# The memory's keys and values, made in an opening stage and reloaded for attention

## The reference

```python
def memory_kv(mem, g_mem, w_mkv):
    mk, mv = split_cols(rmsnorm(mem, g_mem) @ w_mkv, (D_MODEL, D_MODEL))   # 256 x 1024 each
x = x + concat([o_dn, o_ssm]) @ w_out                  # gated delta net | Mamba2, both from rmsnorm(x, g_mix) @ w_in
x = x + memory_cross_attention(rmsnorm(x, g_xattn), mem_k, mem_v, w_xq, w_xo)   # q = c @ w_xq; softmax(q k^T / 16) v; @ w_xo
x = x + peer_ffn(rmsnorm(x, g_ffn), ...)               # 128^2 experts, top 16 of 8 heads
y = rmsnorm(x, g_final)
```

## Time and profile before

| | us |
|---|---|
| median of three runs | 5662.15 |
| profiled execution | 5645.43 |
| its span, from the first to the last instruction | 5643.6 |
| loads before the norm of x | 0 to 18.9 |
| norm of x and gates, until the delta net's first load | 18.9 to 91.5 |
| memory's keys and values | 2151.8 to 2252.8 |

### The profile page before, as it was taken

How to read it: one execution, slowest core, us unless ns; L and a number is a source line. 1 busy time by engine, 2 the same in 40 slices (tenths; PEclk the granted TensorE clock), 3 DMA queues, 4 the chain that set the end, 5 groups by cost and what they waited for, 6 DMA issues and landing times. The chain is left out here.

```text
span 5643.6 us, 75351 instructions
## 1 busy us (share of the span) xinstructions
PE 4734.4 (84%) x28237; PEld 4252.3 (75%) x28237; DVE 3211.3 (57%) x6524; ACT 1561.6 (28%) x2965; POOL 1733.4 (31%) x999
## 2 busy tenths in 40 slices
PE   5999999997878586777683666799999999999996
PEld 3777777775656485757683556799999999999996
DVE  2344444442555311221219999577778877777787
ACT  1233222222232211111200444233333333333332
POOL 0111111110111221202210434455555555555552
PEclk8999999997989798898886888899999999999998
DMA  1000000000111302141220244888888888888885
GB/s 66 24 27 27 24 23 27 27 13 35 47 39 39 141 34 82 58 148 37 94 79 25 75 134 119 283 287 291 284 290 295 289 287 289 299 287 281 289 297 194
DMA packets 299961, 802.45 MB, mean 142 GB/s; under 512 B 43584, under 2 KB 188992, under 8 KB 245696
## 3 DMA queue, kind: packets, MB, share of 16 engines
q0 software_dynamic: 55296, 402.68, 20.2%
q1 hardware_dynamic: 207552, 350.36, 18.0%
q10 hardware_dynamic: 36864, 46.15, 2.5%
HBM read 709.22 MB, written 89.89 MB: 142 GB/s over the span
## 5 line engine op out<-in xcount | busy, mean ns | idle before, releaser
L126 PE MATMUL psum_banks<-f_dense_hi,exp_u_hi 128*128 128x352 f32 x2048 | 665.7, 325 | 77.0 <-POOL exp_u_lo L2212 59.6
L2221 POOL DMA_INDIRECT residual<-in_peer_rows,pick_index x384 | 515.6, 1343 | 574.4 <-DVE psum_banks L2430 508.5
L2418 DVE CUSTOM_DVE_ANT_0 residual<-residual,f_rows 128x1024 f32<-128x1024 f32 x384 | 659.8, 1718 | 45.1 <-DMA residual<-in_peer_rows,pick_index 44.4
L126 PE MATMUL psum_banks<-exp_hidden_hi,exp_v_hi 128*128 128x352 f32 x2048 | 661.7, 323 | 7.8 <-issue 7.1
L127 PE MATMUL psum_banks<-f_dense_lo,exp_u_hi 128*128 128x352 f32 x2048 | 661.9, 323 | 0.0
L128 PE MATMUL psum_banks<-f_dense_hi,exp_u_lo 128*128 128x352 f32 x2048 | 661.7, 323 | 0.0
L127 PE MATMUL psum_banks<-exp_hidden_lo,exp_v_hi 128*128 128x352 f32 x2048 | 659.9, 322 | 0.0
L128 PE MATMUL psum_banks<-exp_hidden_hi,exp_v_lo 128*128 128x352 f32 x2048 | 659.7, 322 | 0.0
L476 PE MATMUL psum_banks<-x_normed,dn_weights 128*128 128x384 f32 (+1 forms) x1536 | 528.6, 487 | 13.1 <-DMA dn_conv_w<-in_dn_conv_w 13.1
L2430 DVE SCALAR_TENSOR_TENSOR psum_banks<-residual,exp_coefs,psum_banks 128x1024 f32<-128x1024 f32 x381 | 487.3, 1279 | 0.0
L784 POOL TENSOR_TENSOR dn_block<-dn_lower,dn_level_masks 128x1152 f32<-128x1152 f32 x56 | 146.8, 2628 | 1005.2 <-DVE dn_lower L862 892.8
(11 more groups left out here) (480 smaller groups left out, 9348.0 us busy)
## 6 DMA issues: line engine op xcount, KB each, us to landing
exp_stage<-in_peer_u SPq DMA_DIRECT2D x128, 512.0 KB, 4.8
exp_stage<-in_peer_v SPq DMA_DIRECT2D x128, 512.0 KB, 3.8
exp_gates<-expert_gates ACTq DMA_DIRECT2D x256, 176.0 KB, 4.5
expert_gates<-route_gates SPq DMA_DIRECT2D x5, 8192.0 KB, 31.2
dn_weights<-in_w_dn SPq DMA_DIRECT2D x8, 2048.0 KB, 7.3
retrieval_q<-w_pq_stage SPq DMA_DIRECT2D x16, 576.0 KB, 2.8
residual<-retrieval_q SPq DMA_DIRECT2D x9, 1024.0 KB, 5.9
heads<-mixed_heads SPq DMA_DIRECT2D x16, 544.0 KB, 8.8
```

Source lines behind the costliest of these rows:

```text
L126: nc.tensor.matmul(out, w[0], x[0], start=start, stop=False)
L2221: nc.gpsimd.indirect_dma_start(slot[:, n % SLOTS, :, :].rearrange("p x n -> p (x n)"), None, d["peer_rows"], bass.IndirectOffsetOnAxis(ap= ...
L2418: nc.vector.tensor_tensor_reduce(u, u, xg[:, g, :], 1.0, 0.0, ALU.mult, ALU.add, dots[:, r:r + 1]).then_inc(dotted.sem, 1)
```

## The change

`opening` takes the place of the first loads, the norm of x, `gates` and `memory_kv`, in one phase with one block. SyncE issues three constants, x tile by tile (a semaphore each), memory, the other constants, four pieces (512 KB each) of the keys' weight and four of the values', and then one more piece whenever TensorE has used one. The keys' products are plain float32. The values' matmuls run piece by piece of the weight, into four banks at once. Keys and values go to the outputs and once more to DRAM (`kept_k`, `kept_v`), and the phase waits for all four stores. The query projection takes the two reloads as `prefetch`, and the prompt's attention waits for them before its first scores. The norms and the gates' arithmetic are as before.

```diff
+def opening(nc, bank, xn, const, names, d, kept, tab):
+    STREAM = 4
...
+            def _(sp_):
+                for n in early:                      # ident, ones, gains
...
+                for k in range(KT):
+                    sp_.dma_start(x[:, k, :], d["xT"][k]).then_inc(x_loaded[k].sem, 16)
+                sp_.dma_start(mn[:, :, :], d["memT"]).then_inc(mem_loaded.sem, 16)
...
+                for j in range(KT):
+                    if j >= STREAM:
+                        sp_.wait_ge(k_product.sem, k_product.at(j - STREAM + 1))
+                    sp_.dma_start(wk[:, j % STREAM, :, :], d["w_mk"][j]).then_inc(wk_loaded[j % STREAM].sem, 16)
+                    if j == STREAM - 1:
+                        for k in range(STREAM):
+                            sp_.dma_start(wv[:, k, :], d["w_mv"][:, k, :]).then_inc(wv_loaded[k].sem, 16)
+                for k in range(STREAM, KT):
+                    sp_.wait_ge(v_step.sem, v_step.at(k - STREAM + 1))
+                    sp_.dma_start(wv[:, k % STREAM, :], d["w_mv"][:, k, :]).then_inc(wv_loaded[k % STREAM].sem, 16)
+                sp_.wait_ge(k_taken.sem, k_taken.at(KT))
+                for to in kept[0]:
+                    sp_.dma_start(to, kT[:, :, :]).then_inc(mem_stored.sem, 16)
+                sp_.wait_ge(v_taken.sem, v_taken.at(2 * MT))
+                for to in kept[1]:
+                    sp_.dma_start(to, v_out[:, :, :]).then_inc(mem_stored.sem, 16)
+                sp_.wait_ge(mem_stored.sem, mem_stored.at(len(kept[0]) + len(kept[1])))
...
+                def mem_keys(j):
+                    pe.wait_ge(wk_loaded[j % STREAM].sem, wk_loaded[j % STREAM].at(j // STREAM + 1))
+                    if j >= 2:
+                        pe.wait_ge(k_taken.sem, k_taken.at(j - 1))
+                    for k in range(KT):
+                        mm = nc.tensor.matmul(bank[6 + j % 2][:, 0:MEM], wk[:, j % STREAM, k, :], mn[:, k, :], start=(k == 0), stop=(k == KT - 1))
+                    mm.then_inc(k_product.sem, 1)
...
-            memory_kv(nc, bank, const, d, out, mkT, mv)
+            mem_loaded = Signal(nc, part, "mem_loaded", 2, 16)
...
-                linear(nc, bank, "w_xq", cn, d["w_xq"], KT, KT, T, "store", qx)
+                linear(nc, bank, "w_xq", cn, d["w_xq"], KT, KT, T, "store", qx,
+                       prefetch=[(mkT[:, :, :], kept_k, mem_loaded), (mv[:, :, :], kept_v, mem_loaded)])
```

More of the change, by code:

```diff
@@ new lines, in opening @@
+        x_loaded = [signal(f"x_loaded{k}", 1, 16) for k in range(KT)]
+        mem_loaded = signal("mem_loaded", 1, 16)
+        wk_loaded = [signal(f"w_mem_k_loaded{r}", 1, 16) for r in range(STREAM)]
+        wv_loaded = [signal(f"w_mem_v_loaded{r}", 1, 16) for r in range(STREAM)]
+        padded, zeroed = signal("padded"), signal("zeroed")
+        squared, added, summed, mean_ready, root_ready, rstd_ready, spread, normed = (
+            signal(n) for n in ("squared", "added", "summed", "mean_ready", "root_ready", "rstd_ready", "spread", "normed"))
@@ new lines, in mem_values @@
+                def mem_values(k):
+                    pe.wait_ge(wv_loaded[k % STREAM].sem, wv_loaded[k % STREAM].at(k // STREAM + 1))
+                    if k == 0:
+                        pe.wait_ge(k_taken.sem, k_taken.at(KT))
+                    for m in range(MT):
+                        for half in range(2):
+                            mm = nc.tensor.matmul(V_BANKS[2 * m + half][:, :], mn[:, k, P * m:P * m + P], wv[:, k % STREAM, 512 * half:512 * half + 512],
+                                                  start=(k == 0), stop=(k == KT - 1))
+                    mm.then_inc((v_product if k == KT - 1 else v_step).sem, 1)
@@ new lines, in _ @@
+                mm.then_inc(msummed.sem, 1)
+                pe.wait_ge(rstd_ready.sem, 1)
+                for t in range(NC):
+                    mm = nc.tensor.matmul(bank[1 + t // 3][:, P * (t % 3):P * (t % 3) + P],
+                                          rstd[:, t:t + 1].to_broadcast([P, P]), ident[:, :], start=True, stop=True)
+                mm.then_inc(spread.sem, 1)
+                pe.wait_ge(mrstd_ready.sem, 1)
+                for t in range(MT):
+                    mm = nc.tensor.matmul(bank[4][:, P * t:P * t + P], mrstd[:, t:t + 1].to_broadcast([P, P]), ident[:, :], start=True, stop=True)
@@ L276, in _ @@
                 mm.then_inc(projected.sem, 1)
+                for j in range(4, 6):
+                    mem_keys(j)
                 pe.wait_ge(vec.sem, vector_at["decays"])
@@ L283, in _ @@
                 mm.then_inc(cumulated.sem, 1)
+                for j in range(6, KT):
+                    mem_keys(j)
+                for k in range(KT):
+                    mem_values(k)
             @block.scalar
@@ L300, in _ @@
                 nc.scalar.activation(z[:, :, :], u[:, :, :], ACT.Ln).then_inc(sca.step(), 1)
+                for j in range(4, 6):
+                    take_key(j)
                 act.wait_ge(vec.sem, vector_at["sums"])
@@ new lines, in _ @@
+                v.wait_ge(spread.sem, 1)
+                for k in range(KT):
+                    for c, (a, n) in enumerate(CHUNKS):
+                        op = nc.vector.scalar_tensor_tensor(xn[:, k, a:a + n], x[:, k, a:a + n], gain[:, k:k + 1],
+                                                            bank[1 + c][:, 0:n], ALU.mult, ALU.mult)
+                    op.then_inc(normed.sem, 1)
+                v.wait_ge(sca.sem, scalar_at["sigmoid"])
+                v.wait_ge(small_loaded.sem, small_loaded.at(len(names)))
```

173 lines of the change are left out of this document (103 added, 70 removed).

## The result

The changed kernel takes 5596.96 us (median of four, 5595.28 to 5607.59), the kernel before 5662.53 in the same comparison: a ratio of 0.9888, 95% interval 0.9869 to 0.9906. The forecast was 5596. A later comparison gave 5601.34 against 5657.58, 0.9900 (0.9884 to 0.9917).

What follows compares the result with a forecast made beforehand. The prediction took both changed places to be serial stretches where one engine or a load is waited for. Removal -101.0 plus opening +35.0 gave -66, from median 5662.15 to 5596 us, range 5583 to 5609.

Steps and rivals of the forecast that it cites:

- Removal, -101.0: Between output projection and attention norm: the whole memory stage leaves its place, saving 101.0 us.
- Step 1: Opening's loads: x issued earlier, squares and additions under the loads, additions ending at 18.3 instead of 32.0, saving 13.7 us.
- Step 2: Opening's two norms in one order: memory normed until 36.4, then x until 48.6, 4.6 us earlier than before.
- Steps 3 and 4: Opening's keys and gates: three keys until 48.9, gates until 64.4, keys 4 and 5 free, cumulation from 77 to 81.
- The 2 us added for a start at 1.2 GHz: Opening's first three keys: 2 us added to 10.4 because TensorE begins at 1.2 GHz after idling.
- Step 5: Opening's bare tail: keys 6 and 7 6.9, values 27.7, then copies, stores, stage end; delta net at 126.5, opening +35.0 us.
- the clock rises late: Rival: opening's first three keys and cumulation run at 1.2 GHz, 8.4 and 4 us more, 5608 us; chance 0.13.
- Weights and reload at nothing: Opening's weight stream hidden by four pieces in flight, and the reload hidden in the query projection: both cost nothing.
- the rival's 26: Rival: in the opening, weight pieces come one at a time, eight later pieces showing 3.2 us each, +26, 5622; chance 0.04.

Runs made afterwards that it cites:

- Experiment 2: Kernel before with only the opening merged and x squared as it lands, memory made in its old place and way: 5642.58 us against 5654.92, ratio 0.9967.
- experiment 8: Changed kernel with key 6 also made ahead of the cumulation, so no wait there: 5589.01 us; the changed kernel once more beside it: 5601.34 us.
- the ring of two: Changed kernel with two pieces of each weight in flight instead of four: 5592.43 us.
- experiments 5 and 7: Changed kernel with keys and values stored once: 5600.50 us; that plus keys 6 and 7 between cumulation pairs, early copies, delta net's first weights loaded in the opening: 5580.82 us.
- experiment 6: Changed kernel with the matmuls of keys 6 and 7 set between the cumulation's pairs instead of behind it: 5588.29 us, ratio 0.9883.
- the ring of one: Changed kernel with one piece of each weight in flight instead of four: 5678.19 us against 5656.38 for the kernel before.

## Why the prediction was right, step by step

*Removal, -101.0.* From the delta net's first load to the end of the output projection's last addition it was 2059.05 us before and 2058.36 after; then 1.26 to the attention's norm, 1.2 forecast. The whole stage went, and nothing hidden came out.

*Step 1, loads.* The additions end at 18.25, 18.3 forecast; the last square starts at 15.61, the tile was put at 15.8. Experiment 2 confirms the 13.7 as 13.9.

*Step 2, norms.* Memory normed at 35.8 (36.4 forecast), x at 47.9 (48.6): the order as foreseen, some tenths quicker at each hand-over.

*Steps 3 and 4.* Keys 0 to 2 take 12.7 (12.5), the gates 15.6 (15.5), the transposes start at 67.79 (67.8), the cumulation at 76.89 (77) and it ends at 80.9 (81). That keys 4 and 5 cost nothing is right but for what they are too short for: 1.25 us of wait remain. The 2 us added for a start at 1.2 GHz have the right size, but not the sign that was given for them. The copies of keys 0 and 1 start when each key is done:

```profile
41.74 0.39 ACT L390 ACTIVATE open_mem_keys<-psum_banks 128x256 f32<-128x256 f32 x1 [13.75 <-PE psum_banks L324]
45.19 0.39 ACT L390 ACTIVATE open_mem_keys<-psum_banks 128x256 f32<-128x256 f32 x1 [3.07 <-PE psum_banks L324]
```

So key 0 took 5.9 us from 35.85 on and key 1 took 3.45, while the granted clock reads 1.00 through both, and had read so through TensorE's wait of 3.40 us ahead of key 0. The gates of before, "begun cold" for the prediction, show the same: 5 passes in their first 3 us, 4 in the single microsecond from 59, at a granted 1.00 throughout. What slowed these first matmuls isn't shown.

*Step 5.* Here is the term that was mis-sized: keys 6 and 7, 6.9 forecast, took 8.84, with a granted clock of 0.79, 0.50 and 0.86 in the three stretches of 2 us from 80 (experiment 8). The rival "the clock rises late" named the wait of over 1 us ahead of the cumulation as what spoke for it. The clock was up early, but fell once more behind that wait, at a price of 1.9 (about 5 in the second execution) instead of the rival's 12. Experiment 8 shows the step without it: key 7 in 3.70, the values 3.7 us earlier, of which 0.5 was there before the transposes. The values' 27.7 was exact. Copies, stores and stage end took 9.6 from 118.07 (10.3 forecast). Sum of the opening +36.2, forecast +35.0.

*Weights and reload at nothing.* No wait on a weight. The price without the ring was far above the rival's 26: twelve pieces were waited for instead of eight, 3.7 us each instead of 3.2, and TensorE also worked some 27 us longer (+69.2 in all). The reload: the third query weight comes 0.6 us later relative to its stage, and the stretch from the attention's norm to the experts is 1299.3 (1298.2 and 1300.2 in the two profiles of before): hidden. The scores waited for the queries alone, as forecast.

*The whole.* -66 forecast, -65.5 at the attention's norm, -65.6 and -56.2 in the medians. The closeness of the first median to 5596 is in part luck, since the changed kernel itself moves by some us at the clock and more in the experts' stage.

## What to carry to other kernels

Look for stretches where an engine waits for a norm or a scalar chain, and move there work that depends only on inputs; what it costs is then what sticks out of the holes, here 50 us of a stage that took 101 alone. Put enough of it in front of each wait that TensorE doesn't run dry there (one key more ahead of the cumulation took 3.2 us out of the stretch around it), and stream its weights with two or more pieces issued ahead. Judge a change of this size at points that repeat, such as a stage's first load, as well as by the total.

## What the runs showed of the hardware that was not expected

- A wait of TensorE of 1.25 us between dense work was followed by 1.2 GHz in both executions of the changed kernel, from the stretch at 80 in one and at 78 in the other; by the stretches' means it was there for about 3.4 us in one and 10 in the other. Three more kernels with the wait fell too (the ring of two, experiments 5 and 7). Without the wait (two kernels) 1.00 held until the values ended, across the same narrow matmuls and a wait of 0.56. One kernel with the wait (experiment 6) kept 1.00 until a second wait of 2.0, and with the ring of one a fall came 8.9 us after the last wait. What sets the start and the length of the fall stays open.
- Key 0 took 5.9 us and key 1 3.45, the same matmuls, with a granted clock of 1.00 over both.
- Experts' stage: 2050 to 2082 us with the same instructions, and with it 1718 to 1833 ns for a dot product of 1024 columns on VectorE.
